# VectorE turns the latent rows by 32x32 blocks; ScalarE's high parts of the last queries and of the keys move behind other work

## What is computed

```python
h = x @ w_in[l]
(qa, ka, va, ga, iq, ik, iw, c_q, c_kv, k_rope, gb) = _split_cols(h)
qa = _rope(qa.reshape(B, S, A_HEADS, A_HEAD_DIM), positions)
ka = _rope(ka.reshape(B, S, A_HEADS, A_HEAD_DIM), positions)
...
o_a = _dsa_branch(qa, ka, va, iq, ik, iw) * jax.nn.silu(ga)
o_b = _mla_branch(c_q, c_kv, k_rope, q_norm_g[l], w_uq[l], kv_norm_g[l],
                  w_ukv[l], positions) * jax.nn.silu(gb)
...
# inside _mla_branch
q = (_rmsnorm(c_q, q_norm_g) @ w_uq).reshape(B, S, B_HEADS, B_NOPE_DIM + B_ROPE_DIM)
kv = (_rmsnorm(c_kv, kv_norm_g) @ w_ukv).reshape(B, S, B_HEADS, B_NOPE_DIM + B_V_DIM)
```

## Time and profile before

| | |
|---|---|
| runs | 283.96, 284.26, 284.38 us, median 284.26 |
| profiled execution | 284.04 us, of which the span 282.2 |
| TensorE products busy | 273.8 us, 97% of the span |
| VectorE busy | 232.2 us, 82% |
| GpSimd busy | 188.6 us, 67% |
| ScalarE busy | 149.6 us, 53% |
| granted TensorE clock, mean | 0.991 |

### The profile page before, as it was taken

How to read it: one execution, slowest core, us unless ns; L and a number is a source line. 1 busy time by engine, 2 the same in 40 slices (tenths; PEclk the granted TensorE clock), 3 DMA queues, 4 the chain that set the end, 5 groups by cost and what they waited for, 6 DMA issues and landing times.

```text
span 282.2 us, 5134 instructions
## 1 busy us (share of the span) xinstructions
PE 273.8 (97%) x1664; PEld 228.6 (81%) x1664; DVE 232.2 (82%) x528; ACT 149.6 (53%) x352; POOL 188.6 (67%) x209
## 2 busy tenths in 40 slices
PE   8999999999999999999999999999999999999990
PEld 7999987778888888888888888885778788888890
DVE  2699998989999999999984798668694967986375
ACT  5656534674452576224188696777764774552000
POOL 5898999834199999999935993885799923010012
PEclk9999999999999999999999999999999999999996
DMA  7985543222623396221238652817800000545022
GB/s 240 364 256 172 151 138 130 74 77 74 149 59 93 83 250 190 74 74 44 70 91 211 231 141 78 224 53 270 349 2 2 0 1 2 172 110 168 0 77 74
DMA packets 20874, 35.41 MB, mean 125 GB/s; under 512 B 6928, under 2 KB 9488, under 8 KB 20592
## 3 DMA queue, kind: packets, MB, share of 16 engines
q1 hardware_dynamic: 20272, 34.79, 41.0%
q10 hardware_dynamic: 576, 0.29, 0.4%
HBM read 26.69 MB, written 2.10 MB: 102 GB/s over the span
## 4 chain that ended last, share of the span: by engine, by line
PE 96%; DMA 1%; DVE 1%; DVEq 0%; issue 0%; ACT 0%
PE ps L1320 52%; PE ps L1643 16%; PE ps L1560 6%; PE ps L1521 5%; PE ps L1581 3%; PE ps L1605 3%; PE ps L1503 2%; PE ps L1336 2%; PE ps L1506 2%; PE ps L1430 2%; DMA w_raw<-in_w_in 1%; PE ps L1540 1%; PE ps L1616 1%; PE ps L1439 0%; PE ps L1413 0%; DVEq L255 0%
## 5 line engine op out<-in xcount | busy, mean ns | idle before, releaser
L624 POOL TENSOR_TENSOR w_lo<-w_raw,w_hi 128x512 fp32r<-128x512 f32 (+3 forms) x62 | 83.8, 1374 | 17.4 <-ACT w_hi L770 16.8
L770 ACT ACTIVATE w_hi<-w_raw 128x512 fp32r<-128x512 f32 (+3 forms) x62 | 35.9, 595 | 55.2 <-PE ps L1320 51.9
L881 ACT ACTIVATE probs<-probs,small 128x512 f32<-128x512 f32 (+3 forms) x64 | 35.7, 559 | 23.2 <-DVE small L1150 22.8
L1643 PE MATMUL ps<-wo_hi,oT 128*128 128x512 f32 (+1 forms) x144 | 45.4, 388 | 0.0
L1320 PE MATMUL ps<-w_hi,x_lo 128*128 128x512 f32 (+3 forms) x120 | 43.0, 362 | 0.0
L1320 PE MATMUL ps<-w_lo,x_hi 128*128 128x512 f32 (+3 forms) x120 | 42.9, 361 | 0.0
L1320 PE MATMUL ps<-x_hi,w_hi 128*128 128x512 f32 x96 | 38.0, 396 | 0.0
L1320 PE MATMUL ps<-x_lo,w_hi 128*128 128x512 f32 x96 | 37.4, 390 | 0.0
L1320 PE MATMUL ps<-x_hi,w_lo 128*128 128x512 f32 x96 | 37.4, 389 | 0.0
L1320 PE MATMUL ps<-w_hi,x_hi 128*128 128x512 f32 (+2 forms) x84 | 32.1, 382 | 0.0
L1643 PEld LDWEIGHTS ps<-wo_hi,oT 128*128 128x128 f32 x144 | 25.9, 189 | 5.2 <-issue 0.2
(11 more groups left out here) (196 smaller groups left out, 631.3 us busy)
## 6 DMA issues: line engine op xcount, KB each, us to landing
w_raw<-in_w_in SPq DMA_DIRECT2D x20, 512.0 KB, 3.6
kaT_swap<-kaT SPq DMA_DIRECT2D x8, 256.0 KB, 3.8
w_raw<-in_w_out SPq DMA_DIRECT2D x4, 512.0 KB, 4.8
wo_early<-in_w_out SPq DMA_DIRECT2D x4, 512.0 KB, 4.8
wo_raw_b<-in_w_out SPq DMA_DIRECT2D x4, 512.0 KB, 4.8
x_res<-in_x SPq DMA_DIRECT2D x4, 512.0 KB, 7.1
x_raw<-in_xT SPq DMA_DIRECT2D x3, 512.0 KB, 6.4
out_y<-y SPq DMA_DIRECT2D x6, 256.0 KB, 2.4
```

The source lines that it names most:

```text
L624: pool.tensor_tensor(w_lo[:, s, 0:n], w_raw[:, s, 0:n], w_hi[:, s, 0:n], ALU.subtract).then_inc(w_lo_ready, 1)
L770: act.activation(dst, w_raw[:, s, 0:n], ACT.Copy).then_inc(w_hi_ready, 1)
L881: act.activation(probs[:, u % NPROBS, 0:N], probs[:, u % NPROBS, 0:N], ACT.Exp, bias=neg_max[:, u % 8:u % 8 + 1], scale=-1.0, accum_out=ro ...
L1643: ins = mm(out_ps(i, b), oT[i % 2][:, o, k, :], w[:, wcols], start=first, stop=final)
```

## The change

Four things move together.

1. The twelve transposes leave TensorE. VectorE turns each of the four row blocks of `lat_tok` (128 tokens x 384 columns) in 32x32 squares into `lat_st`, one instruction each, directly behind the indexer's scores and ahead of the angles for the rows. SP then puts the squares in their places with 16 DMAs (`lat_st` to `lat_pT`), queued between the turn of the queries and the next load of weights.
2. ScalarE's `latT_hi` and VectorE's `latT_lo` read `lat_pT` in SBUF in place of the PSUM banks.
3. The high parts of the last two query heads move from ahead of ScalarE's value copies to behind them.
4. The high parts of all eight key heads move behind the high part of the last weight chunk (61), in one piece, still ahead of the copies of gate B. TensorE's first scores wait for the keys head by head and for the swapped keys pair by pair, in place of for all at once.

The diff, without the lines that only rename or declare:

```diff
@@ -170,6 +170,8 @@
     ik_lo = sb("ik_lo", 88, [P, SEQ], f32r)
     latT_hi = sb("latT_hi", 80, [P, QL_T + 1, SEQ], f32r)
     latT_lo = sb("latT_lo", 86, [P, QL_T + 1, SEQ], f32r)
+    lat_st = sb("lat_st", 102, [P, 4, QL_T + 1, TT, SQ])
+    lat_pT = sb("lat_pT", 108, [P, QL_T + 1, TT, 4, SQ])
     oT0 = sb("oT0", 80, [P, 2, KT, P], f32r)
     wo_early = sb("wo_early", 80, [P, 2, 2, BANK])
     tmp = sb("tmp", 94, [P, 2, BANK])
...
@@ -375,6 +377,10 @@
                 eng.wait_ge(side_read[m], 2)
             else:
                 eng.wait_ge(acc_read[m], acc_seen(TT * ACC_GROUP[g] + m) + 2)
+
+        def latT_raw(t):
+
+            return lat_pT[:, t].rearrange("p m a q -> p (m a q)")
 
         def low_part(eng, src, dst, h):
...
@@ -493,6 +499,10 @@
                         wait_tok(sp, G_Q, b)
                     sp.wait_ge(relu_used, (TT - 1) * IDX_HEADS)
                     turn(qT, qT_turned, q_turned)
+                    sp.wait_ge(lat_turned, TT)
+                    for c in range(4):
+                        for a in range(4):
+                            sp.dma_start(lat_pT[SQ * c:SQ * (c + 1), :, :, a], lat_st[SQ * a:SQ * (a + 1), c]).then_inc(lat_placed, 16)
                 if q == K_TURN_AT:
                     for b in range(4):
                         wait_tok(sp, G_K, b)
...
@@ -502,7 +512,7 @@
                 sp.wait_ge(k_low_ready, h + 2)
                 for a in range(2):
                     sp.dma_start(kaT_swap[A_DIM * a:A_DIM * (a + 1), h:h + 2, :].bitcast(f32),
-                                 kaT[A_DIM * (1 - a):A_DIM * (2 - a), h:h + 2, :].bitcast(f32)).then_inc(kaT_swapped, 16)
+                                 kaT[A_DIM * (1 - a):A_DIM * (2 - a), h:h + 2, :].bitcast(f32)).then_inc(kaT_swapped[h // 2], 16)
             def place(a, dst, blk, done):
...
@@ -777,7 +787,8 @@
 
                     act.wait_ge(relu_used, (TT - 1) * IDX_HEADS)
                     act.wait_ge(kpe_blocked, 1)
-                    act.wait_ge(side_ready, F_LAT + QL_T + 1)
+                    act.wait_ge(side_ready, F_END)
+                    act.wait_ge(lat_turned, TT)
                 if g == G_LAT:
                     for m in range(TT):
                         act.wait_ge(side_ready, m + 1)
...
@@ -815,10 +826,9 @@
 
             def evac_lat_hi():
                 act.wait_ge(norm_g_loaded, 32)
+                act.wait_ge(lat_placed, 16 * 16)
                 for t in range(QL_T + 1):
-                    n = F_LAT + t
-                    act.wait_ge(side_ready, n + 1)
-                    act.activation(latT_hi[:, t, :], side[:, n % 4], ACT.Copy,
+                    act.activation(latT_hi[:, t, :], latT_raw(t), ACT.Copy,
                                    scale=gq[:, t:t + 1] if t < QL_T else gkv).then_inc(lat_hi_ready, 1)
 
             def high_parts(src, dst, i, done):
...
@@ -853,13 +863,17 @@
                         act.wait_ge(rows_arg_ready, 1)
                         act.activation(sin_rows[:, :], ang_rows[:, :], ACT.Sin, scale=freq_sb[:, 1:2])
                         act.activation(cos_rows[:, :], turns_rows[:, :], ACT.Sin, bias=half_pi, scale=-1.0).then_inc(rows_ready, 1)
-                    if g == G_V and j >= Q_HIGH_AT:
+                    if g == G_V and Q_HIGH_AT <= j < Q_HIGH_AT + A_HEADS // 2 - 1:
                         act.wait_ge(q_rotated, j - Q_HIGH_AT + 1)
                         high_parts(qT, qaT, j - Q_HIGH_AT, q_hi_ready)
-                    if g == G_GB and K_HIGH_AT <= j < K_HIGH_AT + A_HEADS // 2:
+                    if g == G_GB and nxt + j == C_OUT - 1:
                         act.wait_ge(k_rotated, A_HEADS // 2)
-                        high_parts(kT, kaT, j - K_HIGH_AT, k_hi_ready)
+                        for i in range(A_HEADS // 2):
+                            high_parts(kT, kaT, i, k_hi_ready)
                 evac_group(g)
+                if g == G_V:
+                    act.wait_ge(q_rotated, A_HEADS // 2)
+                    high_parts(qT, qaT, A_HEADS // 2 - 1, q_hi_ready)
                 if g == G_Q:
                     for i in range(4 * (KT - 4), 4 * (KT - 3)):
                         relu_unit(i)
...
@@ -1091,6 +1105,11 @@
                                            op1=ALU.add).then_inc(relu_used, 1)
             dve.wait_ge(relu_used, (TT - 1) * IDX_HEADS)
 
+            dve.wait_ge(lat_normed, 2 * TT)
+            for m in range(TT):
+                V.transpose(lat_st[:, :, :, m].rearrange("p c t q -> p t c q"),
+                            lat_tok[:, m, 0:Q_LORA + KV_LORA].rearrange("p (t c q) -> p t c q", c=4, q=SQ)).then_inc(lat_turned, 1)
+
             dve.wait_ge(dve_step, rows_turns)
             reduce_angle(ang_rows[:, :], turns_rows[:, :], rows_arg_ready)
...
@@ -1109,10 +1128,9 @@
 
 
             for t in range(QL_T + 1):
-                n = F_LAT + t
                 dve.wait_ge(lat_hi_ready, t + 1)
-                V.scalar_tensor_tensor(out=latT_lo[:, t, :], in0=side[:, n % 4], scalar=gq[:, t:t + 1] if t < QL_T else gkv,
-                                       in1=latT_hi[:, t, :], op0=ALU.mult, op1=ALU.subtract).then_inc(side_read[n % 4], 2)
+                V.scalar_tensor_tensor(out=latT_lo[:, t, :], in0=latT_raw(t), scalar=gq[:, t:t + 1] if t < QL_T else gkv,
+                                       in1=latT_hi[:, t, :], op0=ALU.mult, op1=ALU.subtract).then_inc(lat_lo_ready, 1)
 
             for b in range(4):
                 wait_tok(dve, G_K, b)
...
@@ -1431,14 +1449,6 @@
                             if j == 2 and a == rounds - 1:
                                 ins.then_inc(side_ready, 1)
 
-            def lat_transposes():
-                pe.wait_ge(lat_normed, 2 * TT)
-                for t in range(QL_T + 1):
-                    bank = fill(F_LAT + t)
-                    for m in range(TT):
-                        ins = nc.tensor.transpose(bank[:, m * P:(m + 1) * P], lat_tok[:, m, t * P:(t + 1) * P], ident[:, :])
-                    ins.then_inc(side_ready, 1)
-
             def beside(g, k):
 
                 if g == G_Q:
...
@@ -1447,9 +1457,6 @@
                             idx_transposes(n)
                     elif k >= 3:
                         idx_logits(4 * (k - 3))
-                if g == G_V and k == KT - 1:
-                    lat_transposes()
-
 
             pe.wait_ge(warm_ready, 1)
             for _ in range(NWARM):
...
@@ -1465,8 +1472,8 @@
 
 
 
-            for n in range(F_LAT, F_LAT + QL_T + 1):
-                pe.wait_ge(side_read[n % 4], seen(n) + 2)
+            pe.wait_ge(lat_hi_ready, QL_T + 1)
+            pe.wait_ge(lat_lo_ready, QL_T + 1)
             npe = B_HEADS * ROPE_D
             wait_chunk(C_UQP + 1)
             for m in range(TT):
...
@@ -1498,11 +1505,12 @@
                     if u == 0:
                         pe.wait_ge(q_hi_ready, A_HEADS)
                         pe.wait_ge(q_low_ready, A_HEADS)
-                        pe.wait_ge(k_hi_ready, A_HEADS)
-                        pe.wait_ge(k_low_ready, A_HEADS)
+                    if u < BLOCK_UNITS:
+                        pe.wait_ge(k_hi_ready, h + 1)
+                        pe.wait_ge(k_low_ready, h + 1)
                     mm(ps_s[:, b, 0:N], qaT[:, h, t], kaT[:, h, 0:N], start=True, stop=False)
-                    if u == 0:
-                        pe.wait_ge(kaT_swapped, 16 * A_HEADS)
+                    if u < BLOCK_UNITS and h % 2 == 0:
+                        pe.wait_ge(kaT_swapped[h // 2], 16 * 2)
                     ins = mm(ps_s[:, b, 0:N], qaT[:, h, t], kaT_swap[:, h, 0:N], start=False, stop=True)
                 else:
                     if u == NU_A:
```

More of the change, by code:

```diff
@@ L269, in build @@
         xres_loaded = [sem(f"xres_loaded{i}") for i in range(2)]
-        kaT_swapped, stored = sem("kaT_swapped"), sem("stored")
+        kaT_swapped, stored = [sem(f"kaT_swapped{i}") for i in range(A_HEADS // 2)], sem("stored")
         kpe_blocked, qpe_blocked = sem("kpe_blocked"), sem("qpe_blocked")
@@ L289, in build @@
         lat_ms_ready, lat_rs_ready = sem("lat_ms_ready"), sem("lat_rs_ready")
-        lat_normed, lat_hi_ready = sem("lat_normed"), sem("lat_hi_ready")
+        lat_normed, lat_hi_ready, lat_lo_ready = sem("lat_normed"), sem("lat_hi_ready"), sem("lat_lo_ready")
+        lat_turned, lat_placed = sem("lat_turned"), sem("lat_placed")
         qpe_rotated = sem("qpe_rotated")
@@ L324, in build @@
         LOGITS_USED = [sum(len(heads) for m, heads in LOGITS[:i + 1]) for i in range(len(LOGITS))]
-        F_LAT = F_LOGIT + len(LOGITS)
-        F_END = F_LAT + QL_T + 1
+        F_END = F_LOGIT + len(LOGITS)
         A_QPE = (NG - 1) * TT
@@ L1689 @@
 POS_ROWS_AT, Q_TURN_AT, K_TURN_AT = 6, 19, 23
-ROWS_AT, Q_HIGH_AT, K_HIGH_AT = 2, 3, 2
+ROWS_AT, Q_HIGH_AT = 2, 3
 Q_LOW_AT = 45
```

## The result

The changed kernel takes 288.41 us in the median of six runs (287.07 to 289.51), the kernel before 284.32 (six runs on the same chip). The ratio is 1.0141, 95% interval 1.0108 to 1.0174: about 4.1 us slower. Run again on another chip it was 288.26 against 284.6, ratio 1.0135 (1.0109 to 1.0161). The forecast was 286.2 with a range of 283.4 to 287.8: the direction was right, but the time is 2.2 us above the forecast and 0.6 above the range. For the second chip 288.4 (287.0 to 289.5) had been written down before it ran.

What follows compares the result with a forecast made beforehand. TensorE was taken to bound the kernel (busy 97% of the span), with ScalarE's key parts and gate copies nearly late. 284.04 - 1.35 + 3.3 = 286.0, with 0.22 for the median 286.2 us; range 283.4 to 287.8.

Steps and rivals of the forecast that it cites:

- Transposes off TensorE, -1.35: Between the value products and the last gate group, removing twelve transposes saves TensorE 1.35 us.
- VectorE's four transposes, 2.0 us: Ahead of VectorE's angle reduction, four 128x384 transposes take 2.0 us, all of it a delay of the keys.
- rival (a): Keys late by the transposes alone, low parts at 0.72: TensorE waits 1.1 us, 284.0, not slower; chance 0.17.
- Latent low parts 1.70 each, +3.1: On VectorE, three latent low parts reading SBUF beside GpSimd take 5.1 us in place of 2.0.
- Keys at 146.5, gate copy's end at 152.4, wait 3.3: At the projections' end, late keys delay ScalarE's first gate copy to 152.4; TensorE, ready at 149.1, waits 3.3 us.
- The three w_hi that now stand ahead, -1.4: On ScalarE, three w_hi now precede the key parts instead of standing between them, taking 1.4 us off the gate copy's delay.
- It waits 3.3 us; behind it ... TensorE's tiles of six 128x256 products every 0.7, so no second wait.: After TensorE's 3.3 us wait, gate copies come every 0.65 and its tiles every 0.7, so no further wait.
- SP's sixteen transfers: In SP's queue, they take 10 to 16 us; the next weight load goes out at 83 to 89, cost 0.
- The value copies: On ScalarE, directly behind w_hi, the first ends near 104.3, before TensorE wants its bank at 105.57; cost 0.
- Rival (c): GpSimd's backlog starts later, through crowded query turns or late sine rows; with 3 us, 288; chance 0.10.
- Rival (b): Nobody is late: the keys have more room, the whole 1.35 us gain stays, 282.9; chance 0.11.

Runs made afterwards that it cites:

- keysonly: The kernel before with only the eight key parts moved in one row behind the last w_hi; 285.85 us, ratio 1.0050.
- turn4: The kernel before with VectorE's four 128x384 transposes added, their output unread, TensorE keeping its own twelve; 284.63 us, ratio 1.0004.
- spreadb: The kernel before with one pair of key parts behind the last w_hi and three behind the rotary query copies; 289.73 us, ratio 1.0191.
- spreadq: The changed kernel with three of four key-part pairs behind the rotary query copies and the last query parts back ahead of the value copies; 284.80 us, ratio 1.0005.
- psumlow: The changed kernel with VectorE's three latent low parts reading a PSUM bank of left-over numbers instead of SBUF; 284.49 us, ratio 1.0000.
- oldkeys: The changed kernel with the key parts back in their old place, two per chunk from chunk 58 on; 286.58 us, ratio 1.0069.
- holdw: The changed kernel with one added wait: ScalarE waits for the rotated keys ahead of w_hi of chunk 59; 286.69 us, ratio 1.0076.
- fill: The changed kernel with 14 dummy 128x512 products on TensorE in the gap before the 128x256 products; 286.70 us, ratio 1.0086.

## Why the prediction was right in direction and wrong in size

- **Transposes off TensorE, -1.35.** Right. From the first product of the value group to the first of gate B (83.81 to 128.69 in the kernel before) are 44.88 or 44.89 us in the four profiles with the transposes and no wait there (before, keysonly, turn4, spreadb), and 43.51 or 43.52 in eight of the nine without them; the ninth is spreadq: 1.36 less. "Free" shows it less well (149.51 in the mean of those eight, 150.56 of the four, 1.05 earlier), since the traces already differ by up to 1.5 us at the first value product.
- **VectorE's four transposes, 2.0 us.** Measured 1.96. That all of it is a delay of the keys was wrong: aligned by the first value product, the latents' low parts start 1.4 to 1.5 later in turn4 and in the changed kernel, and turn4 absorbed the rest, because each us by which the adds slip behind GpSimd's block makes them shorter. The working knew this effect and used it for the sum, but not for rival (a).
- **Latent low parts 1.70 each, +3.1.** Right: 5.17 for three, 0.74 each from PSUM in psumlow. By the exclusive lock of the Trainium skill ("SBUF — State Buffer", contention) they would have taken 2.1 each; the changed kernel shows 1.77, one every 1.70, while GpSimd's subtractions beside them went from 1.30 to 1.62. The measurement decides: both slow down, and neither stands still for the whole of the other's instruction.
- **Keys at 146.5, gate copy's end at 152.4, wait 3.3.** ScalarE starts at 147.26 and the gate copy at 152.49, in a trace that was 0.6 late; the wait was 3.39 and 3.32. Right to 0.1.
- **The three w_hi that now stand ahead, -1.4.** Counted as a saving of the move, this is wrong in sign, though the sum that contained it came out. By itself the move costs 1.3 (keysonly); in the changed kernel it frees GpSimd to subtract beside the adds, which makes the keys 2.8 us later (147.26 against 144.42) and costs 1.3 of wait and part of the clock's fall (oldkeys, holdw). The working let GpSimd slow the adds, but never set the old order beside the new: by its own rates (1.70 beside GpSimd, 0.7 alone) the keys would be ready at 144.4 in the old order; oldkeys measured 144.42. So it blamed the transposes and the latents for about 1.3 of the 3.3 us of wait that this edit makes.
- **The step that failed: "It waits 3.3 us; behind it ... TensorE's tiles of six 128x256 products every 0.7, so no second wait."** There was no second wait, but the tiles came every 1.28: the sum had no term for what a wait of this length does to TensorE's clock. It measured 2.4 us in one profile, 1.5 in the other, 1.6 in the median of the runs (against fill). With it: 284.3 - 1.35 + 3.35 + 1.6 + 0.2 behind it = 288.1, against 288.3 measured. The kernel before waits no longer than 0.3 us between its start and its last product, but its trace does show the fall. The page's row of the granted clock, in slices of 7 us (9 is 90% or more of full speed), ends in a 6:

```profile
PEclk9999999999999999999999999999999999999996
```

  TensorE's last product ends at 275.25; the granted clock is still 1.00 from 276 to 277 and 0.50 from 277.5 on, a little over 2 us after TensorE stopped. A wait of 3.3 us is longer than that. With a bound of half the speed for the 24 products behind the wait (2.9 us more) the sum would have read 286.2 to 289.1.
- **SP's sixteen transfers** took 12.46 and the load went out at 86.0, inside 83 to 89, at no cost. **The value copies** came at 104.38 (the trace 0.6 late), at no cost; that the old order would just miss its moment is borne out by the 0.3 us of spreadq. **Rival (c)** did not come about: GpSimd's rotation of the queries begins at 77.43, 0.6 later, as all of that trace, and waits for the DMA. **Rival (a)** is met by psumlow in number (a wait of 1.16 against its 1.1), but not in cause: there nobody waits for the keys, but the key parts stand behind the last `w_hi`. The working's own numbers give this floor: chunk 61 at 143.9, its `w_hi` 0.63, eight parts 5.2 and a copy 0.65 make 150.4, 1.3 after 149.1. **Rival (b)**, that the whole 1.35 stays, was thus not open to this kernel, however early the keys.

## What to carry to other kernels

Price a new wait of the busiest engine twice: its length, and the work behind it at half the clock if a trace shows the clock falling behind a stop of that length, be it only at the kernel's end; the second term was here half as large as the first, and it varied from run to run. Work taken off TensorE is only a gain if the engine that receives it is not the one that feeds the next buffer: here 1.36 us were saved, and some 5 came back through the chain keys, key parts, gate copy. And before moving an instruction out of another's way, ask whom its waiting kept quiet: ScalarE's wait for the keys had kept GpSimd off VectorE's adds.

## What the runs showed of the hardware

- Granted clock 0.50 for 3.0 to 5.4 us behind waits of 3.3 to 3.4 us (two of two profiles), for 3.4 us behind one of two waits of 2.1 us, not behind 1.2 us (two profiles). In the kernel before it falls a little over 2 us after TensorE's last product. Products of 256 columns then start 0.21 apart instead of 0.12.
- Four VectorE adds of 128x512 with both inputs in SBUF: 2.48 us beside a quiet GpSimd, 5.21 beside a subtracting one. A SCALAR_TENSOR_TENSOR of that size beside a busy GpSimd: 1.77 with both inputs in SBUF (changed kernel), 0.74 with one in PSUM (psumlow).
- A 128x384 fp32 block transpose on VectorE took 0.49 (1.96 for four).
- An execution outlasts its span by 1.76 to 1.96 us in 63 runs of the kernel before, and by 2.7 to 3.9 in half of the runs of spreadq; the cause is open.
